# Latent attention over the prompt: transposes of a step ahead of the scores of the step three ahead

## The chip, the cores and the metric

The kernel runs on one core of one Trainium2 chip. The metric is the device time of one execution in microseconds (us); the kernel before takes 2766.6 us, the median of three runs (2764.68 to 2768.49).

## The reference, cut to what matters

The program is one inference step of a two-layer encoder: a layer with latent attention (MLA) and a layer with stick-breaking attention, each followed by an MLP. It works on a prompt of 1024 tokens and on 8 streams of 16 new tokens. The change touches only the latent attention over the prompt. For each of 8 heads it computes:

```
scale = (MLA_NOPE + MLA_ROPE) ** -0.5
s = (einsum('bqhd,bkhd->bhqk', q_nope, k_nope)
     + einsum('bqhr,bkr->bhqk', q_rope, k_rope)) * scale
mask = (k_pos[None, :] // CHUNK) <= (q_pos[:, None] // CHUNK)      # CHUNK = 64
s = where(mask, s, -inf)
p = softmax(s, axis=-1)
out = einsum('bhqk,bkhd->bqhd', p, v)
```

The outputs are float32. The kernel splits each float32 operand into a high and a low part, and a product is three matmuls (`product`, lines 77 to 79 of the kernel).

## The kernel before, in words

`mla_attention_stage` (line 582) handles the heads in four pairs, one pair per iteration of `pairs`. Within a pair there are `STEPS = 16` steps: step n is head n // 8 of the pair and query tile q = n % 8 of 128 tokens. Because of the mask, tile q needs only the first (q + 1) x 128 keys, so the steps grow from 128 to 1024 keys and start again at step 8. Each step passes through these pieces:

- **Scores** (`scores(n)`, TensorE, lines 923 to 938): three matmuls for the non-rotary part and two for the rotary part on each chunk of up to 512 keys, then one small matmul that adds the mask (L936). They are written to one of two score buffers, `score[n % 2]`, so `scores(n + 3)` first waits until the exponential of step n + 1 has read that buffer.
- **Maximum** (`maximum(n)`, VectorE, L838 and L841): the negated row maximum, and its product with the scale.
- **Exponential** (`exponential(n)`, ScalarE, L750): reads the scores, writes `prob[n % 3]`, and sums the rows.
- **Normalise** (`normalise(n)`, VectorE, L847 and L849): the reciprocal of the sum, and the probabilities times it, in place.
- **Transposes** (`transposes(n)`, TensorE, L946): they wait for `normed`, the signal of the normalise of the same step, and turn the q + 1 blocks of 128 x 128 in tasks of up to four into one of three banks. A task needs its bank emptied by the low split of the task three before.
- **High and low split** (ScalarE L761, VectorE L859): copy a task out of its bank into `pt`.
- **Values** (`values(g)`, TensorE, lines 950 to 959): once for every two steps (a group), 3 x (last_q + 1) matmuls of 256 columns, that is 6, 12, 18 and 24 for the four groups of a head; the result is copied out by ScalarE (L768).

Four value projections and `scores(0)` to `scores(2)` stand ahead of the 16 steps, and the projections of the next pair follow steps 13 to 15 (`TAIL`). At step 6 ScalarE and VectorE also split the raw weights of the next pair (L737, L742, L826, L831), in all pairs but the last.

Every engine runs its instructions in the order in which they are written, and the orders are written out by hand. On VectorE the loop over n is: `maximum(n + 3)`, `normalise(n + 1)`, the weights at step 6, `transposed_lo(n)`. On ScalarE it is: `exponential(n + 2)`, the weights at step 6, `transposed_hi(n)`, and the output of a group at even n. The change leaves both orders alone. SP's queue holds the stores of a group (L662), the loads of the next weights (L568, L570) and of the rotary queries (L656); GpSimd does nothing in this stage.

Of the kernel before, what the change touches and what calls it, by code (L numbers as in the profile page):

```python
# [74 lines left out]
def product(pe, out, w, m, start, stop, resumed=False):  # L75

    pe.matmul(out, w[0], m[0], start=start, stop=False, skip_group_check=resumed)  # L77
    pe.matmul(out, w[0], m[1], start=False, stop=False, skip_group_check=resumed)  # L78
    return pe.matmul(out, w[1], m[0], start=False, stop=stop, skip_group_check=resumed)  # L79
# [447 lines left out]
def score_columns(q):  # L527


    used = (q + 1) * P  # L530
    keys = max(used, 2 * P)
    first = P if keys == 640 else 0
    chunks, at = [], first
    while at < first + keys:
        end = min(512 * (at // 512 + 1), first + keys)
        chunks.append((at, end - at, at - first))
        at = end
    return first, chunks, used


def transpose_tasks(n):


    q = n % NPT
    order = [(q, 0)] + [(k, k + 1) for k in range(q)] if q % 2 else [(k, k + 1) for k in range(q + 1)]
    return [order[i:i + 4] for i in range(0, len(order), 4)]


def tasks_before(n):

    return sum(len(transpose_tasks(m)) for m in range(n))


STEPS = 2 * NPT
# [27 lines left out]
def mla_attention_stage(nc, io, scratch, raw, wq, smp_in, q_rope_out, o_out):  # L582
# [12 lines left out]
    with nc.cleanup_on_exit(), ExitStack() as ctx:  # L595
# [38 lines left out]
        def task_bank(m):  # L634

            return bank[:, 4 + m % 3, :]

        def project_bank(n):

            return bank[:, n % 4 if n < QK - 2 else 4 + n % 3, :]  # L640

        def pairs(engine, body):

            with engine.Fori(0, PAIRS - 1) as i:
                body(i, False)
            body(PAIRS - 1, True)
# [240 lines left out]
        @block.tensor  # L887
        def _(pe):
            proj.start(pe)
            pv_done.start(pe)  # L890

            def project(i, n, first=False):
                if n < 4 and not first:
                    exp_done.wait(pe, STEPS * i + n // 2 - 1)
                elif n >= 4:

                    reused = n - 4 if n < QK - 2 else n - 3 if n >= QK + 1 else None
                    if reused is not None:
                        proj_lo.wait(pe, PROJ * i + reused + 1)
                    elif n < QK:  # L900
                        t_lo.wait(pe, T_TASKS * i)
                ps = project_bank(n)
                if n < Q_TASKS:
                    a, c = n // 3, n % 3
                    for k in range(QT):
                        last = product(pe, ps[:, 0:384], [w[:, k, a, :] for w in wq],
                                       [x[:, k, c * 384:(c + 1) * 384] for x in cqT], k == 0, k == QT - 1)
                elif n < Q_TASKS + K_TASKS:
                    a, c = (n - Q_TASKS) // 2, (n - Q_TASKS) % 2
                    for k in range(CT):  # L910
                        last = product(pe, ps, [w[:, k, a, 0:NOPE] for w in wkv],
                                       [x[:, k, c * 512:(c + 1) * 512] for x in ckvT], k == 0, k == CT - 1)
                else:
                    for j in range(2):
                        t = 2 * (n - Q_TASKS - K_TASKS) + j
                        for k in range(CT):
                            last = product(pe, ps[:, j * GQ:(j + 1) * GQ],
                                           [x[:, k, t * P:(t + 1) * P] for x in ckvT],
                                           [w[:, k, :, NOPE:] for w in wkv], k == 0, k == CT - 1)
                last.then_inc(proj.sem, 1)  # L920

            def body(i, is_last):
                def scores(n):
                    a, q = n // NPT, n % NPT
                    tile = slice(q * P, (q + 1) * P)
                    exp_done.wait(pe, STEPS * i + n - 1)
                    first, chunks, used = score_columns(q)
                    for at, width, key in chunks:
                        out = score[n % 2][:, at:at + width]
                        keys = slice(key, key + width)  # L930
                        product(pe, out, [x[:, a, tile] for x in qn], [x[:, a, keys] for x in kn], True, False)
                        pe.matmul(out, qr[:, a, tile], krT[0][:, keys], start=False, stop=False)
                        last_chunk = (at, width, key) == chunks[-1]
                        last = pe.matmul(out, qr[:, a, tile], krT[1][:, keys], start=False, stop=not last_chunk)
                    end = first + used
                    last = pe.matmul(score[n % 2][:, end - P:end], io["ident16"][:], io["chunk_mask"][:],  # L936
                                     start=False, stop=True)
                    last.then_inc(s_done.sem, 1)

                def transposes(n):  # L940
                    normed.wait(pe, STEPS * i + n + 1)
                    for j, task in enumerate(transpose_tasks(n)):
                        m = tasks_before(n) + j
                        t_lo.wait(pe, T_TASKS * i + m - 2)
                        for c, (k, _) in enumerate(task):
                            last = pe.transpose(task_bank(m)[:, c * P:(c + 1) * P],  # L946
                                                prob[n % 3][:, k * P:(k + 1) * P], ident[:])
                        last.then_inc(t_done.sem, 1)

                def values(g):  # L950
                    a, last_q = g // 4, 2 * (g % 4) + 1
                    t_lo.wait(pe, T_TASKS * i + tasks_before(2 * g + 2))
                    o_done.wait(pe, GROUPS * i + g)
                    order = [(last_q, 0)] + [(k, k + 1) for k in range(last_q)]
                    for k, slot in order:
                        last = product(pe, bank[:, 7, 0:GQ],
                                       [x[:, k, a * VDIM:(a + 1) * VDIM] for x in v],
                                       [x[:, slot, :] for x in pt[g % 2]], k == last_q, k == last_q - 1)
                    last.then_inc(pv_done.sem, 1)

                proj_lo.wait(pe, PROJ * i + QK - 3)
                qr_in.wait(pe, 16 * (i + 1))
                scores(0)
                proj_lo.wait(pe, PROJ * i + QK - 2)
                scores(1)
                for n in range(QK, PROJ):
                    project(i, n)
                scores(2)
                for n in range(STEPS):
                    if n + 3 < STEPS:  # L970
                        scores(n + 3)
                    if n == 0:
                        proj_lo.wait(pe, PROJ * (i + 1))
                        zero_done.wait(pe, 4)
                    if n == NPT + 1:
                        values(NPT // 2 - 1)
                    transposes(n)
                    if n % 2 == 0 and n >= 2 and n != NPT:
                        values(n // 2 - 1)
                    if n == min(TAIL) and not is_last:  # L980
                        w_lo.wait(pe, 2 * (i + 2))
                    for m in TAIL.get(n, ()) if not is_last else ():
                        project(i + 1, m)
                values(GROUPS - 1)
                for m in TAIL[STEPS] if not is_last else ():
                    project(i + 1, m)

            w_lo.wait(pe, 1)
            for n in range(QK):
                if n == Q_TASKS:  # L990
                    w_lo.wait(pe, 2)
                project(0, n, True)

            pairs(pe, body)
    return w_four

# [1937 lines left out]
class SbSchedule:  # L2934
# [6 lines left out]
    STEPS = 2 * PAIR_STEPS  # L2941
# [798 lines left out]
```

## Time and profile before

| what | us |
|---|---|
| median of three runs | 2766.6 |
| the profiled execution's own time | 2768.86 |
| its span | 2765.2 |
| TensorE busy, whole span | 2667.1 (96%) |
| VectorE busy | 1733.0 (63%) |
| ScalarE busy | 1156.7 (42%) |

The span is what the profiler saw of one execution, from the first instruction of the program to the last; the time of the execution lies some 3.7 us above it. TensorE's busy time is of matmuls whose ends are modelled: a matmul is shown for longer than the distance to the next one, because they are pipelined. The latent attention over the prompt takes the stretch from 163 to 457 us of the span.

### The profile page before, as it was taken

The page shows a single profiled execution, that of the slowest core. Times are in us where ns is not written, and L with a number is a line of the kernel's source. Part 1 is how long each engine was busy: PE and PEld are TensorE (multiplying, and loading weights), DVE is VectorE, ACT ScalarE, POOL GpSimd, SP SyncE. Part 2 cuts the span into 40 slices and gives each one's busy share as a digit, 9 for nine tenths or more (in the row PEclk, how much of TensorE's full clock was granted, in tenths as well). Part 3 has the DMA queues.
Part 4 walks back from the last instruction along what each step waited for, and adds up shares of the span by engine and source line. Part 5 has one row for each costly group of instructions (what it writes and reads, how often), then busy time and mean ns, then how long its engine had stood idle before and what let it go on. Part 6 is the DMA issues. An engine that isn't in the chain of part 4 may idle for free. (4 is left out here: it accounts for less than half of the span.)

```text
span 2765.2 us, 40402 instructions
## 1 busy us (share of the span) xinstructions
PE 2667.1 (96%) x14531; PEld 2236.8 (81%) x14531; DVE 1733.0 (63%) x2331; ACT 1156.7 (42%) x2260; POOL 732.0 (26%) x627
## 2 busy tenths in 40 slices
PE   7989998999999999999899999998999999999998
PEld 6878887788888878888798887776878888788886
DVE  5656666376555688888410008887485555788887
ACT  4334445343333333344322219998343333333433
POOL 3200001135544400000221116666045544300001
PEclk9999999999999999999999999999999999999999
DMA  4211122514444573533234437763324444654342
GB/s 150 86 61 46 46 79 89 184 60 153 137 137 144 170 256 125 162 122 118 80 128 151 155 102 194 172 173 121 111 95 145 137 137 145 235 181 164 127 154 100
DMA packets 285877, 368.81 MB, mean 133 GB/s; under 512 B 25984, under 2 KB 205696, under 8 KB 285696
## 3 DMA queue, kind: packets, MB, share of 16 engines
q1 hardware_dynamic: 285696, 366.42, 41.7%
q8 instruction: 110, 1.80, 0.3%
q14 instruction: 71, 0.58, 0.1%
HBM read 242.19 MB, written 124.16 MB: 132 GB/s over the span
## 5 line engine op out<-in xcount | busy, mean ns | idle before, releaser
L2342 DVE TENSOR_TENSOR x<-m_ps,x 128x1024 f32<-128x1024 f32 x224 | 273.3, 1220 | 91.9 <-PE m_ps L79 91.8
L2051 POOL TENSOR_TENSOR m_u<-m_u,m_u 128x512 f32<-128x512 f32 x128 | 179.6, 1414 | 349.0 <-DVE m_u L2185 344.0
L1998 POOL TENSOR_SCALAR m_stat<-m_stat 128x1 f32<-128x1 f32 x36 | 12.1, 335 | 831.6 <-ACT m_sqjunk L1942 667.2
L2173 DVE TENSOR_TENSOR m_z<-m_ps,m_part 128x512 f32<-128x512 f32 x96 | 66.3, 691 | 143.8 <-PE m_ps L79 143.5
L1800 ACT COPY m_part<-m_ps 128x512 f32<-128x512 f32 x96 | 56.4, 588 | 205.2 <-PE m_ps L79 205.2
L2161 DVE TENSOR_TENSOR m_up<-m_upr,m_up 128x512 fp32r<-128x512 f32 x128 | 87.9, 707 | 28.5 <-ACT m_up L1787 28.5
L3300 ACT ACTIVATE e_b<-e_ps 128x512 f32<-128x512 f32 (+3 forms) x192 | 95.9, 500 | 12.1 <-PE e_ps L3518 11.6
L1787 ACT CAST m_up<-m_upr 128x512 fp32r<-128x512 f32 x128 | 75.7, 615 | 57.9 <-PE m_ps L79 57.9
L3302 ACT ACTIVATE e_ps<-e_ps 128x512 f32<-128x512 f32 (+3 forms) x192 | 96.3, 501 | 0.0
L2031 POOL TENSOR_TENSOR m_uprS<-m_upr 128x512 f32<-128x512 f32 x62 | 94.6, 1526 | 5.0 <-DVE m_upS3l L2161 4.9
L3583 PE MATMUL e_ps<-ident,e_b 128*128 128x128 f32 x576 | 94.7, 274 | 0.7 <-POOL e_b L3398 0.6
L2185 DVE SCALAR_TENSOR_TENSOR m_u<-m_z 128x512 f32<-128x512 f32 x96 | 90.1, 939 | 2.3
L2859 ACT COPY d_rows<-d_ps 128x512 f32<-128x512 f32 x36 | 21.1, 587 | 163.1 <-PE d_ps L79 163.1
L1138 POOL TENSOR_TENSOR c_wo0l<-c_wo0r,c_wo0h 128x1024 fp32r<-128x1024 f32 x1 | 2.4, 2352 | 322.5 <-ACT c_wo0h L1112 322.5
L2161 DVE TENSOR_TENSOR m_upS2l<-m_uprS,m_upS2h 128x512 fp32r<-128x512 f32 x32 | 33.9, 1061 | 84.7 <-ACT m_upS2h L1787 84.7
L77 PE MATMUL m_ps<-m_up,m_t8h 128*128 128x256 f32 x256 | 72.5, 283 | 0.9 <-DVE m_t8l L2123 0.9
L79 PE MATMUL m_ps<-m_up,m_t8l 128*128 128x256 f32 x256 | 72.4, 283 | 0.0
L78 PE MATMUL m_ps<-m_up,m_t8h 128*128 128x256 f32 x256 | 72.4, 283 | 0.0
L3583 PEld LDWEIGHTS e_ps<-ident,e_b 128*128 128x128 f32 x576 | 65.3, 141 | 6.8 <-ACT e_pt L3327 0.7
L3327 ACT COPY e_pt<-e_ps 128x512 f32<-128x512 f32 (+3 forms) x128 | 67.1, 524 | 0.0
L3398 POOL TENSOR_TENSOR e_b<-e_b,e_r0long 128x1024 f32<-128x1024 f32 (+3 forms) x32 | 53.8, 1682 | 42.0 <-DVE e_r0long L3454 41.9
L3398 POOL TENSOR_TENSOR e_b<-e_b,e_r1long 128x1024 f32<-128x1024 f32 (+3 forms) x32 | 53.3, 1666 | 43.8 <-DVE e_r1long L3454 43.8
(1192 smaller groups left out, 9185.8 us busy)
## 6 DMA issues: line engine op xcount, KB each, us to landing
scratch_u<-m_u SPq DMA_DIRECT2D x224, 256.0 KB, 2.1
m_ur<-scratch_u SPq DMA_DIRECT2D x208, 256.0 KB, 2.7
m_upr<-in_mlp_w_up SPq DMA_DIRECT2D x32, 1024.0 KB, 5.9
m_wr<-in_mlp_w_down SPq DMA_DIRECT2D x64, 512.0 KB, 6.6
scratch_x<-x SPq DMA_DIRECT2D x18, 512.0 KB, 2.6
x<-scratch_x SPq DMA_DIRECT2D x8, 1024.0 KB, 9.5
scratch_qr<-a_qrst SPq DMA_DIRECT2D x9, 512.0 KB, 3.4
a_x<-in_x_prompt SPq DMA_DIRECT2D x8, 512.0 KB, 5.0
```

Of the source, the lines that this page charges most:

```text
L77: pe.matmul(out, w[0], m[0], start=start, stop=False, skip_group_check=resumed)
L78: pe.matmul(out, w[0], m[1], start=False, stop=False, skip_group_check=resumed)
L1787: act.copy(up[n][0], up_source(n, p)).then_inc(up_hi.sem, 1)
L2031: pool.tensor_tensor(up_sum[n][:], up_source(ins[0], p), up_source(ins[1], p), ALU.add if n == "S1" else ALU.subtract).then_inc(up_summed. ...
L2051: pool.tensor_tensor(u_st[out][:], u_st[a][:], u_st[b][:], op).then_inc(u_summed.sem, 1)
L2161: dve.tensor_tensor(up[n][1], up_source(n, p), f32(up[n][0]), ALU.subtract).then_inc(up_lo.sem, 1)
L2185: dve.scalar_tensor_tensor(out=u_st[slot][:], in0=src[:], scalar=0.0, in1=src[:], op0=ALU.max, op1=ALU.mult).then_inc(u_done.sem, 1)
L2342: dve.tensor_tensor(out, bank[:, at:at + 2, :], out, ALU.add).then_inc(summed.sem, 1)
L3300: act.activation(take(n)[:, key:key + used], z[:, 0:used], ACT.Sigmoid, scale=SB_SCALE).then_inc(taken.sem, 1)
L3302: act.activation(z[:, 0:used], z[:, 0:used], ACT.Sigmoid, scale=-SB_SCALE).then_inc(kept.sem, 1)
L3398: pool.tensor_tensor(b, b, remaining(n)[:, -used:], ALU.mult).then_inc(weighted.sem, 1)
L3583: t = pe.transpose(task_bank(m)[:, c * P:(c + 1) * P], take(n)[:, k * P:(k + 1) * P], ident[:])
```

## The change: what it does

In TensorE's program, the call `scores(n + 3)` moves from the head of the loop body to behind `transposes(n)`. It then also comes behind the wait for the last value projection at n = 0 and behind `values(3)` at n = 9, and still ahead of `values(n // 2 - 1)` at the other even steps. No instruction is added or removed, and the order of no other engine changes.

```diff
                 scores(2)
                 for n in range(STEPS):
-                    if n + 3 < STEPS:
-                        scores(n + 3)
                     if n == 0:
                         proj_lo.wait(pe, PROJ * (i + 1))
                         zero_done.wait(pe, 4)
                     if n == NPT + 1:
                         values(NPT // 2 - 1)
                     transposes(n)
+                    if n + 3 < STEPS:
+                        scores(n + 3)
                     if n % 2 == 0 and n >= 2 and n != NPT:
                         values(n // 2 - 1)
                     if n == min(TAIL) and not is_last:
```

## Rows read from the trace of the kernel before

**Rows 1.** The page, part 1: busy time, share, and instructions of each engine.

```profile
PE 2667.1 (96%) x14531; PEld 2236.8 (81%) x14531; DVE 1733.0 (63%) x2331; ACT 1156.7 (42%) x2260; POOL 732.0 (26%) x627
```

**Rows 2.** Windows: stretch, length, engines' busy time (instructions), TensorE clock, DMA share, GB/s.

```profile
163.00:457.00 294.00, 285.31 (x1888) 259.51 (x1888) 183.49 (x419) 141.01 (x327) 0.00 (x0) 0.99 0.17 53
263.00:297.00 34.00, 32.97 (x225) 28.82 (x224) 26.32 (x65) 19.81 (x47) 0.00 (x0) 1.00 0.06 19
```

**Rows 3.** Waits of TensorE, 163 to 457: who for whom, total us, times, longest.

```profile
PE b_ps L77 <- ACT b_p L750: 2.6, 8, 0.4
...
PE b_ps L946 <- DVE b_p L849: 1.5, 5, 0.6
PE b_ps L946 <- DVE b_pt1l L859: 1.1, 3, 0.4
```

**Rows 4.** Timeline, end of scores(6), step 3: start, us, engine, line, operation, tiles, shape.

```profile
272.72 0.23 PE L936 MATMUL b_ps<-chunk_mask,ident 128*128 128x128 bf16 x1
272.78 0.60 PE L946 MATMUL b_ps<-ident,b_p 128*128 128x128 f32 x4
...
272.99 1.09 DVE L838 TENSOR_REDUCE b_stat<-b_ps 128x1 f32<-128x896 f32 x1 [0.94 <-PE b_ps L936]
...
274.11 0.15 DVE L841 TENSOR_SCALAR b_stat<-b_stat 128x1 f32<-128x1 f32 x1
274.19 0.15 DVE L847 RECIPROCAL b_stat<-b_stat 128x1 f32<-128x1 f32 x1
...
274.37 0.55 DVE L849 TENSOR_SCALAR b_p<-b_p,b_stat 128x640 f32<-128x640 f32 x1
...
274.84 0.69 DVE L859 TENSOR_TENSOR b_pt1l<-b_ps,b_pt1h 128x512 fp32r<-128x512 f32 x1
```

**Rows 5.** Timeline, step 13: a normalise and the transposes that waited for it.

```profile
301.34 0.62 DVE L849 TENSOR_SCALAR b_p<-b_p,b_stat 128x768 f32<-128x768 f32 x1
...
302.02 1.04 PE L946 MATMUL b_ps<-ident,b_p 128*128 128x128 f32 x6 [0.25 <-DVE b_p L849]
```

**Rows 6.** Lines by form, VectorE: busy us, mean ns, idle before; smallest and largest step.

```profile
L838 DVE TENSOR_REDUCE b_stat<-b_ps 128x1 f32<-128x1024 f32 x8 | 9.8, 1225 | 2.2 <-PE b_ps L936 2.2
...
L849 DVE TENSOR_SCALAR b_p<-b_p,b_stat 128x1024 f32<-128x1024 f32 x8 | 6.0, 754 | 0.3
...
L849 DVE TENSOR_SCALAR b_p<-b_p,b_stat 128x128 f32<-128x128 f32 x8 | 2.3, 287 | 0.3
L838 DVE TENSOR_REDUCE b_stat<-b_ps 128x1 f32<-128x128 f32 x8 | 2.3, 284 | 0.0
```

**Rows 7.** Timeline: the first matmul of values(1), and the first matmul after its twelve.

```profile
276.07 0.36 PE L77 MATMUL b_ps<-b_pt1h,b_vh 128*128 128x256 f32 x1
...
277.59 0.28 PE L77 MATMUL b_ps<-b_knh,b_qnh 128*128 128x256 f32 x1
```

**Rows 8.** Timeline, start of the second pair: scores(2) end, last low split, scores(4).

```profile
263.85 0.69 DVE L822 TENSOR_TENSOR b_vl<-b_ps,b_vh 128x512 fp32r<-128x512 f32 x1 [0.75 <-ACT b_vh L732]
...
263.91 0.23 PE L936 MATMUL b_ps<-chunk_mask,ident 128*128 128x128 bf16 x1
...
265.95 0.44 PE L77 MATMUL b_ps<-b_knh,b_qnh 128*128 128x384 f32 x1 [0.42 <-ACT b_p L750]
```

**Rows 9.** Timeline, steps 6 and 7: the weights on VectorE, and the transposes behind.

```profile
282.14 1.22 DVE L826 TENSOR_TENSOR b_wql<-raw_wq,b_wqh 128x1024 fp32r<-128x1024 f32 x1
283.27 1.22 DVE L831 TENSOR_TENSOR b_wkvl<-raw_wkv,b_wkvh 128x1024 fp32r<-128x1024 f32 x1
...
285.15 0.66 PE L946 MATMUL b_ps<-ident,b_p 128*128 128x128 f32 x4 [0.37 <-DVE b_pt1l L859]
```

**Rows 10.** Windows with idle in them; columns as in Rows 2.

```profile
20.00:25.00 5.00, 3.93 (x15) 3.24 (x16) 2.17 (x3) 1.24 (x2) 1.26 (x2) 0.75 0.90 203
30.00:35.00 5.00, 2.69 (x11) 2.22 (x12) 3.12 (x7) 2.36 (x7) 3.31 (x6) 0.78 0.02 3
...
456.00:460.00 4.00, 1.94 (x16) 1.73 (x16) 1.07 (x5) 1.96 (x5) 0.00 (x0) 1.00 0.44 118
```

## The prediction

> **What bounds the kernel now.** I read the page's busy times first, then the windows of the stage, then TensorE's waits in it, then one pair's timeline. TensorE is busy 96% of the span [rows 1], and the stage of the change is no exception: 285.3 of its 294 us [rows 2]. Between its steps TensorE hardly waits: eight waits for an exponential (2.6 us), five for a normalise (1.5), three for an emptied bank (1.1) [rows 3]. So this stage is bound by TensorE's own stream, at the full clock of 2.4 GHz, and whatever makes TensorE wait lengthens the kernel one for one. VectorE is the next busiest, 26.3 us in the 34 us of steps 0 to 12 of a pair [rows 2]. It has room in total, but what matters is when it gets to a normalise.
>
> The timeline shows why there are so few waits. At step 3 the last matmul of scores(6) starts at 272.72. VectorE starts maximum(6) when it has ended, and behind it in its queue normalise(4), which ends at 274.92 [rows 4]. TensorE has transposes(3), scores(7) and values(1) to do before it asks for normalise(4) in transposes(4). The 2 us of VectorE's chain lie beside more than 2 us of matmuls.
>
> **What the change does to that.** It adds and removes no instruction and no DMA; SP's queue and GpSimd are untouched. It moves scores(n+3) behind transposes(n), so after scores(n+3) the next thing that TensorE meets is transposes(n+1), with values between them at even n alone. But transposes(n+1) needs normalise(n+1), which stands in VectorE's queue behind maximum(n+3), which needs the end of scores(n+3). The cover is gone: TensorE finishes a step's scores and then stands still for VectorE's maximum and normalise. Queued behind the waiting transposes are scores(n+4) and all that follows them, and VectorE's next maximum waits for those, so the wait comes back at every step.
>
> **The price of one such wait**, counted from when TensorE could issue its next instruction:
> - 0.21 us until the maximum starts (272.78 to 272.99; the small matmul that ends the scores is still in the pipeline) [rows 4];
> - the maximum: 0.28 us for one tile of 128 keys, 1.23 for eight [rows 6], 0.134 for each tile between (the 1.09 for seven tiles fits [rows 4]);
> - 0.29 us from its end (274.08) to the start of the normalise, with the two small operations in it [rows 4];
> - the normalise: 0.29 us for one tile, 0.75 for eight [rows 6], 0.067 each between (0.55 for five fits [rows 4]);
> - 0.06 us from its end (301.96) to the transposes at 302.02 [rows 5].
>
> So 0.56 + maximum(n+3) + normalise(n+1). At even n the values matmuls are in front of it: twelve took 276.07 to 277.59, 0.127 us each [rows 7], so groups of 6, 12, 18 and 24 cover 0.76, 1.52, 2.28 and 3.04 us. Per pair:
> - n = 0, no values: 0.56 + 0.69 + 0.35 = 1.60
> - n = 1 and 9: 0.56 + 0.82 + 0.42 = 1.80 each
> - n = 2 and 10: 0.56 + 0.96 + 0.49 - 0.76 = 1.25 each
> - n = 3 and 11: 0.56 + 1.09 + 0.55 = 2.20 each
> - n = 4 and 12: 0.56 + 1.23 + 0.62 - 1.52 = 0.89 each
> - n = 5: 0.56 + 0.28 + 0.69 = 1.53
> - n = 6: 0.56 + 0.42 + 0.75 - 2.28, below zero: covered. n = 8 as well (1.60 against the 3.04 of values(3), which now stands directly behind scores(11)).
> - n = 7: 0.56 + 0.55 + 0.29 = 1.40
>
> These are 16.8 us a pair, 67.2 for four. From n = 13 on no scores are left, and nothing changes.
>
> **Smaller terms.** At n = 0 transposes(0) waits for the last value projection's low split, which ends at 264.54, while scores(2) is issued by 263.95 (the mask's matmul starts at 263.91) [rows 8]. Scores(3) covered this before; now it is 0.65 us, 2.6 for four pairs. Where a step has two tasks, the second needs the bank that the previous step's first low split empties; that split (0.69 us [rows 4]) now starts only behind the normalise that has just released the transposes, against 0.4 us for the first four of them: 0.25 us at steps 5, 6 and 13, 3.0 in all. At step 6 the weights (282.14 to 284.49, 2.35 us [rows 9]) stand between normalise(7) and that split. Normalise(7) ends 1.67 us after scores(9), the bank is free at 1.67 + 2.35 + 0.69 = 4.7, and TensorE is there at 2.28 + 0.4 = 2.7: 2.0 us in three pairs, 6.0.
>
> To be taken off: scores(4) and scores(9) no longer wait for an exponential, since the transposes now give it time. The rows have 2.6 us for these eight waits [rows 3]; to each I add 0.17 that the modelled end of the matmul ahead hides (0.23 less 0.06, [rows 4]) and, as an estimate, 0.1 for the start of a matmul that waited (0.44 us where one of 256 columns in the stream takes 0.28 [rows 7, 8]; part of that is its 384 columns): 4.8. The old waits at steps 7 and 13 are inside the new ones: 0.37 + 0.17 three times [rows 9] and about 0.4 four times [rows 5], 3.2 together. Off: 8.0.
>
> Sum at full clock: 67.2 + 2.6 + 3.0 + 6.0 - 8.0 = 70.8 us.
>
> **The clock.** The trace has stretches with idle in them at either level. From 20 to 25 and from 30 to 35 us the granted clock was 0.75 and 0.78, with TensorE busy 3.93 and 2.69 of 5 us; from 456 to 460 it stayed at 1.00 with 1.94 of 4 [rows 10]. The steps 0 to 12 of a pair will have some 33 us of matmuls in 52, with waits of up to 2.2 us, so both are possible. Bounds: no fall at all, nothing; the half clock of 1.2 GHz throughout these steps, 33 us more a pair less the 4.3 that longer values would hide, 115 us. A mean clock of 0.75 over 5 us is 2.5 us at half rate; with two thirds of such a stretch in matmuls, and counting a tail of it into the next one, a fall costs about 1.3 us. I take two or three a pair, near the 2.2 us waits and the pairs of 1.6 and 1.8: ten, 13 us. That is nearer to the lower bound, because most of the stretches between waits hold more work than the row that stayed at full clock.
>
> The Trainium skill has a rule that speaks against this change, in TensorE: Matmul & The Clock Gate, section "A second HAM failure mode: psum-queue depth-cycling": short idles of TensorE between groups of matmuls, when they come often, make the clock swing between its two levels. The sum would be 70.8 if it did not bite, and goes towards the upper bound if it did at each step; the trace of before has a stretch on either side, 0.75 and 1.00.
>
> Forecast: 2768.86 + 70.8 + 13 for the profiled execution; the median lies 2.3 below that execution, so 2766.6 + 84 = 2850 us.
>
> **The rivals.**
> - *Values cover every even step, and the bank waits are hidden.* Then only the odd steps pay: 1.80 + 2.20 + 1.53 + 1.40 + 1.80 + 2.20 = 10.9 a pair, 44 in all, 2810 us. For it: the even waits are what is left of a difference. Against: their parts are all measured.
> - *The clock is down in most of the steps.* 71 + 115 = 186 us, 2950. For it: rows at 0.75. Against: the row at 1.00 with half of the time idle.
> - *The other side: faster.* Scores(n+3) wait for the exponential of step n+1, and the transposes ahead of them give ScalarE time; the split of a step also starts earlier. If the transposes found their probabilities ready, the 8.0 us above were gained: 2759. The point from which it decides is 8.0 / 44, 0.18 us for each of the 11 waits of a pair; one alone of the five parts of a wait is 0.21. It would need the normalise to run ahead of the maximum on VectorE, and rows 4 show the written order.
> - *No change*, because a later stage takes the time up: it would need idle time of TensorE behind this stage that does not depend on it, and TensorE is 96% busy over the span [rows 1]. The 2767 of before.
>
> **How the numbers follow.** Forecast, whose own range is 2830 to 2870 (hardly any falls to some twenty of them), 0.76; even steps covered 0.11; clock down in most steps 0.06; faster 0.04; no change 0.03. The range that holds 8 in 10 runs from 2818, between forecast and first rival, to 2878. What can be told from no change here is about 0.2%, 5.5 us. Slower 0.93, same 0.03, faster 0.04.
>
> **What would show it.** The stage should be some 84 us longer and everything behind it as long as before. The waits of TensorE should have a new first row, transposes (L946) for the normalise (L849), with about 40 waits and 60 us, the longest near 2 us; the row for the exponential should be gone. In the timeline, at step 3, the end of scores(6), maximum, normalise and the transposes of step 4 should follow one another with no matmul beside them. VectorE's and ScalarE's busy time should be unchanged. The windows of the stage should show a mean clock between 0.9 and 1. The prediction is wrong if transposes(n+1) start less than 1 us after scores(n+3) at odd n, or if the stage grows by less than 50 us.

## The result

The changed kernel takes 2848.0 us (median of four runs, 2841.1 to 2851.5) against 2765.6 us of the kernel before in four runs: slower by 2.94%, ratio 1.0294 with a 95% interval of 1.0278 to 1.0309. The prediction was 2850 us, from 2818 to 2878. The profiled execution took 2851.5 us, its span 2848.1.

The windows show where the time went. First the kernel after: the stage of the change, the rest of the span, and 5 us inside the stage (length, busy PE, PEld, DVE, ACT, POOL, clock, DMA share, GB/s).

```profile
163.50:534.50 371.00, 298.47 (x1888) 266.44 (x1889) 184.28 (x419) 141.84 (x327) 0.00 (x0) 0.98 0.14 42
534.50:2848.10 2313.60, 2249.14 (x11896) 1862.50 (x11896) 1454.39 (x1761) 955.49 (x1802) 693.90 (x562) 0.99 0.45 145
...
285.40:290.40 5.00, 3.49 (x15) 3.23 (x14) 1.47 (x5) 1.20 (x4) 0.00 (x0) 0.66 0.00 0
```

The same two stretches of the kernel before:

```profile
163.30:457.50 294.20, 285.31 (x1888) 259.51 (x1888) 183.49 (x419) 140.71 (x327) 0.00 (x0) 0.99 0.17 53
457.50:2765.20 2307.70, 2244.42 (x11896) 1858.91 (x11896) 1454.35 (x1761) 956.05 (x1802) 693.85 (x562) 0.99 0.46 145
```

The stage is 76.8 us longer. VectorE and ScalarE are as busy as before in it. What follows it is 5.9 us longer in this pair of executions, but the same stretch took 2302.2 to 2314.5 us in the executions below, with no edit behind the stage, so these 5.9 us lie within what one execution differs from another and can't be put down to the change. A granted clock of 1.00 is 2.4 GHz, one of 0.50 is 1.2 GHz. The stage opens at the lower level in both kernels, behind a wait of 3.8 us before and 4.0 us after (L802): before from 163.3 to 169.3, after from 163.5 to 167.6. TensorE's waits in the stage (who for whom, total, times, longest) answer to [rows 3]:

```profile
PE b_ps L946 <- DVE b_p L849: 61.7, 45, 2.0
PE b_ps L946 <- DVE b_pt1l L859: 5.4, 3, 1.8
PE b_ps L77 <- DVEq L802: 4.0, 1, 4.0
PE b_ps L946 <- DVE b_vl L822: 2.1, 4, 0.5
```

The transposes now wait 45 times for the normalise, 61.7 us where it was 1.5; three times for the bank behind the weights, 5.4 us where it was 1.1; four times for the last value projection (L822), which is new. The wait at the stage's opening (L802) stood in the kernel before as well, and so did one of 1.6 us for the values of the last pair. The waits for an exponential are gone. The timeline at step 3 answers to [rows 4]:

```profile
299.15 0.23 PE L936 MATMUL b_ps<-chunk_mask,ident 128*128 128x128 bf16 x1
299.42 1.09 DVE L838 TENSOR_REDUCE b_stat<-b_ps 128x1 f32<-128x896 f32 x1 [2.48 <-PE b_ps L936]
300.54 0.15 DVE L841 TENSOR_SCALAR b_stat<-b_stat 128x1 f32<-128x1 f32 x1
300.61 0.15 DVE L847 RECIPROCAL b_stat<-b_stat 128x1 f32<-128x1 f32 x1
...
300.80 0.55 DVE L849 TENSOR_SCALAR b_p<-b_p,b_stat 128x640 f32<-128x640 f32 x1
...
301.41 0.76 PE L946 MATMUL b_ps<-ident,b_p 128*128 128x128 f32 x5 [2.03 <-DVE b_p L849]
```

End of scores(6), maximum(6), normalise(4), transposes(4): one after the other, and no matmul beside them. VectorE had sat idle for 2.48 us before the maximum, waiting for the scores; then TensorE sat idle for 2.03 us, waiting for VectorE. Before, the same normalise ran beside scores(7).

### The profile page after: what moved, and what is told of

Read it like the earlier page. It is cut to its first block and busy times, and to the rows that moved or that the text cites. A ratio compares the mean times of both kernels' runs of the same rounds, so it can differ in the third digit from the quotient of the medians.

```text
span 2848.1 us, 40402 instructions
## 1 busy us (share of the span) xinstructions
PE 2685.0 (94%) x14531; PEld 2247.3 (79%) x14531; DVE 1734.0 (61%) x2331; ACT 1157.0 (41%) x2260; POOL 731.1 (26%) x627
## 5 line engine op out<-in xcount | busy, mean ns | idle before, releaser
L946 PE MATMUL b_ps<-ident,b_p 128*128 128x128 f32 x288 | 47.7, 287 | 69.2 <-DVE b_p L849 61.7
L838 DVE TENSOR_REDUCE b_stat<-b_ps 128x1 f32<-128x128 f32 (+3 forms) x64 | 48.4, 757 | 103.9 <-PE b_ps L936 103.9
L946 PEld LDWEIGHTS b_ps<-ident,b_p 128*128 128x128 f32 x288 | 31.4, 141 | 79.9 <-DVE b_p L849 41.5
L750 ACT ACTIVATE b_p<-b_ps,b_stat 128x128 f32<-128x128 f32 (+3 forms) x64 | 47.5, 742 | 70.8 <-DVE b_stat L841 70.7
```

The lines of the kernel that those rows point to most:

```text
L946: last = pe.transpose(task_bank(m)[:, c * P:(c + 1) * P], prob[n % 3][:, k * P:(k + 1) * P], ident[:])
```

## The experiments

Each was compared with runs of the kernel before on the same chip; the ratio is to those.

**Is the wait the place in VectorE's queue?** e1 is the changed kernel with two calls swapped:

```diff
-                    if n + 3 < STEPS:
-                        maximum(n + 3)
                     if n + 1 < STEPS:
                         normalise(n + 1)
+                    if n + 3 < STEPS:
+                        maximum(n + 3)
```

> The changed kernel with VectorE's two calls swapped: normalise(n+1) ahead of maximum(n+3); the low split stays last. Theory (TensorE stands still because the normalise is queued behind the maximum of the scores just issued): the 45 waits of transposes for the normalise, 61.7 us, all but vanish. What is left to pay is the low split, still behind the maximum: second tasks of steps 5, 6, 7 and 13 wait for their bank and values(3) for its operands, about 13 us in all, with 2.6 us for the last value projection; 8 us of old waits are gone. So 2769 to 2778. Rival 1 (the clock and the move of the scores themselves cost the time): stays above 2835. Rival 2 (ScalarE, whose exponential now stands between, is what is late): the transposes keep waiting and half or more of the 82 us stays, above 2805.

Measured: 2774.9 us, ratio 1.0031 (1.0018 to 1.0044). The first waits of TensorE in the stage of e1:

```profile
PE b_ps L77 <- DVE b_pt1l L859: 4.6, 5, 1.6
PE b_ps L946 <- DVE b_pt0l L859: 4.6, 13, 0.6
PE b_ps L77 <- DVEq L802: 4.0, 1, 4.0
PE b_ps L946 <- DVE b_pt1l L859: 3.0, 3, 1.0
```

The 61.7 us of waits for the normalise are down to one of 0.6. TensorE's program is the changed one, so neither the move itself nor a late exponential makes the time, nor does the clock fall behind the stage's opening: it is the maximum ahead of the normalise. The remaining 0.3% are waits for the low split (L859), which is still behind the maximum, as expected.

**The swap without the change.** e3 is the kernel before with the same swap.

> The kernel before (scores ahead of transposes) with VectorE's normalise(n+1) ahead of maximum(n+3): the swap alone, as a control for the two above. Theory: the chain behind the scores had its cover there, so the swap is worth next to nothing, within 4 us of 2766 (at most the 1.5 us of waits for a normalise). If the swap were a gain of its own, whatever TensorE's order, it would be here too: 10 us or more below 2766.

Measured: 2767.7 us, ratio 1.0007 (0.9997 to 1.0016). The swap is worth nothing that can be measured where the chain had its cover. It undoes a wait; it is no gain of its own.

**The length of the wait.** e5 is the changed kernel, e6 the one before, both with

```diff
-dve.tensor_reduce(stat[:, n, 0:1], score[n % 2][:, first:first + used], AX.X, ALU.max,
+dve.tensor_reduce(stat[:, n, 0:1], score[n % 2][:, first:first + P], AX.X, ALU.max,
```

> The changed kernel with the maximum taken over the first 128 keys of each row only (the rest of the row is left out of the maximum, nothing else): each maximum costs 0.28 us instead of up to 1.23. Theory: every wait shrinks by what its maximum shrinks: 0.41, 0.54, 0.68, 0.81, 0.89, 0, 0.27, 0.54, 0.68, 0.81 and 0.89 us, 6.5 a pair, 26 in all, so 2822, and the waits for the normalise fall from 61.7 to about 36 us. Rival (a wait has a fixed price, of the handover between engines or of the clock): within 8 us of 2848.

> The kernel before with the same shortened maximum (first 128 keys of each row; the rest is left out of it). Theory: there the maximum lies beside matmuls and is not on the path, so it is worth only the few waits for an exponential: 2760 to 2767. Rival (VectorE's total work counts in this stage): 15 us or more below 2766.

Measured: e5 2810.2 us (1.0160, 1.0140 to 1.0181), e6 2761.6 us (0.9981, 0.9972 to 0.9991). The stage and the first wait of e5:

```profile
162.90:501.50 338.60, 290.30 (x1888) 261.01 (x1889) 154.84 (x419) 140.02 (x327) 0.00 (x0) 1.00 0.15 46
```

```profile
PE b_ps L946 <- DVE b_p L849: 37.2, 37, 1.4
```

About 30 us less of VectorE's work were worth 38 us in the changed kernel and 5 in the one before: the maximum is on the path only with the new order. The waits shrank by 24.5 us, close to the 26 that was forecast; the time shrank by 12 more than forecast. The stage accounts for 32.4 (371.0 to 338.6): the 24.5; some 6 us of clock, by the price below, since behind the stage's opening the changed kernel's clock fell four times and that of e5 never; and 0.6 us, as e5's opening stretch at 1.2 GHz was 2.9 us long instead of 4.1. About 1 us is left open. The rest of the 38 lies outside the stage and is within the spread named above.

**The cover of the values.** e4 puts values ahead of scores(n+3) in the changed kernel.

```diff
                     transposes(n)
-                    if n + 3 < STEPS:
-                        scores(n + 3)
                     if n % 2 == 0 and n >= 2 and n != NPT:
                         values(n // 2 - 1)
+                    if n + 3 < STEPS:
+                        scores(n + 3)
```

> The changed kernel with values ahead of scores(n+3) at even n too, so that nothing lies between scores and the next transposes but at n = 8. Theory (a wait is 0.56 + maximum + normalise less the values in between): at n = 2, 4, 6, 10, 12 the cover of 0.76, 1.52, 1.73, 0.76 and 1.52 us is taken away, 6.3 us a pair or 25 in all, and the values wait some 0.2 us for the low split ahead of them: 28 us over the changed kernel, about 2876, and the waits of transposes for the normalise grow from 61.7 to about 87 us. Rival (the even steps' waits come from something else than this difference, such as the clock): within 10 us of 2848.

Measured: 2897.7 us, ratio 1.0480 (1.0463 to 1.0498), 22 us more than expected. The stage and the first wait of e4:

```profile
163.10:589.40 426.30, 328.15 (x1889) 294.11 (x1889) 184.29 (x420) 144.74 (x327) 0.00 (x0) 0.89 0.12 36
```

```profile
PE b_ps L946 <- DVE b_p L849: 86.1, 49, 2.2
```

The waits came out as worked out, 86.1 us for the 87 forecast: the values matmuls take their own length off a wait. The surplus is the clock, which the expectation left out. Its mean in the stage is 0.89 instead of 0.98: added up over windows of 0.5 us, TensorE spent 96 us at its lower level instead of 18. The stage grew by 55.3 us over the changed kernel, 24.4 of them this wait and 1.2 the wait for the bank; some 30 us are left for 78 more us at 1.2 GHz, nearly 0.4 us each. TensorE's busy time says the same: 328.2 us for the matmuls that took 298.5. (What follows the stage was the shortest of all here, 2302.2 us, so the time shows less than the stage.)

**Only some of the steps.** e7 and e8 put scores(n+3) behind transposes(n) at the odd and at the even steps alone.

```diff
+                    if n + 3 < STEPS and n % 2 == 0:     # e8: n % 2 == 1
+                        scores(n + 3)
                     transposes(n)
-                    if n + 3 < STEPS:
+                    if n + 3 < STEPS and n % 2 == 1:     # e8: n % 2 == 0
                         scores(n + 3)
```

> The change at the odd steps only: scores(n+3) behind transposes(n) at odd n, ahead of them at even n. Behind every odd step then come the scores of the even one, so normalise(n+1) has those beside it; only transposes(n+1) at even n still come soon, behind scores(n+3), transposes(n) and values. Theory: waits of transposes for the normalise at steps 1, 3, 5, 11 and 13 alone, 1.2 + 0.8 + 0.2 + 0.8 + 0.2 us a pair, 13 us in all, and the exponential's waits of before go; 2775 to 2784, no falls of the clock in the stage. Rival (each step at which transposes stand ahead of the scores costs its share of the 82 us, here seven of thirteen): 2805 or more.

> The change at the even steps only: scores(n+3) behind transposes(n) at even n, ahead of them at odd n (behind values(3) at n = 9). Theory: each even step's scores are followed by values and by the next scores, so those waits are covered; but the scores of an odd step n have only transposes(n) between them and transposes(n+1): waits of 1.43, 1.6, 0.7, 0.4, 1.43 and 1.6 us at steps 2, 4, 6, 8, 10 and 12, 7.1 a pair, 29 in all, and 2.6 us for the last value projection; 2790 to 2801. Rival (each step costs its share, here six or seven of thirteen): 2804 to 2810, and waits at the odd steps as well.

Measured: e7 2796.2 us (1.0112, 1.0091 to 1.0133), e8 2807.5 us (1.0147, 1.0128 to 1.0165). Both are above the upper end of their expectation, e7 by 12 us and e8 by 6. e7 lies between its expectation and its rival; e8's time lies in its rival's range (2804 to 2810), so the time alone does not decide, and the waits have to. Their first wait, e7 and then e8:

```profile
PE b_ps L946 <- DVE b_p L849: 17.3, 25, 1.4
```

```profile
PE b_ps L946 <- DVE b_p L849: 34.4, 29, 1.6
```

These were 13 and 29 in the expectations. In the second pair of e7 the steps 1, 3, 5, 11 and 13 wait 1.39, 0.76, 0.29, 0.77 and 0.29 us where 1.2, 0.8, 0.2, 0.8 and 0.2 were given, but step 6 waits 0.73 us too: scores(9), which I took for cover, have 256 keys and are too short. The weights' bank wait of [rows 9] grew from 0.37 to 1.33 us, and values(3) wait 0.87 us for the low split. In the second pair of e8 the steps 2, 4, 6, 8, 10 and 12 wait 1.36, 1.59, 1.01, 0.93, 1.41 and 1.59 us where 1.43, 1.6, 0.7, 0.4, 1.43 and 1.6 were given. Of the odd steps, which the rival has waiting too, 1, 3, 5, 7, 9 and 11 do not wait for the normalise; step 13 does, 0.75 us, and the formula gives it (0.89 less 0.17, see below), but I had left it out. Each of the two also has one fall of the clock in the stage where the expectation of e7 had none. So single waits can be worked out from a formula, but for the two at steps 6 and 8 of e8; the list of who waits was not complete. Time is also not proportional to the number of steps that are changed: what counts is what stands between the scores and the next transposes.

**Can the followers follow?** In e2 VectorE takes the low split ahead of the maximum as well. In e9 ScalarE moves its high split too, and in e10 e9's orders of ScalarE and VectorE meet TensorE's old one. The diff is e9's against the changed kernel; e2 has only the second half of it, with weights_lo ahead of the split.

```diff
 # ScalarE
-                    if n + 2 < STEPS:
-                        exponential(n + 2)
-                    if n == WEIGHTS_AT and not last:
-                        weights_hi(i + 1)
                     if n == NPT + 1:
                         output(NPT // 2 - 1)
                     transposed_hi(n)
+                    if n + 2 < STEPS:
+                        exponential(n + 2)
+                    if n == WEIGHTS_AT and not last:
+                        weights_hi(i + 1)
 # VectorE
-                    if n + 3 < STEPS:
-                        maximum(n + 3)
                     if n + 1 < STEPS:
                         normalise(n + 1)
-                    if n == WEIGHTS_AT and not last:
-                        weights_lo(i + 1)
                     transposed_lo(n)
+                    if n + 3 < STEPS:
+                        maximum(n + 3)
+                    if n == WEIGHTS_AT and not last:
+                        weights_lo(i + 1)
```

> The changed kernel with VectorE's order normalise(n+1), weights at step 6, transposed_lo(n), maximum(n+3). Theory: neither the transposes nor their banks wait for a maximum any longer; the exponential's waits of before (4.8 us) stay gone, the projection's 2.6 us stay. Something like 2758 to 2768, level with the kernel before or a little under it. Rival 1 (clock or the move itself): above 2835. Rival 2 (the maximum, now late behind the split, delays the exponential and with it the scores): a new wait of scores for the exponential of some 1 us at the short steps 5 to 8, 2770 to 2785.

> The changed kernel with all three followers in TensorE's new order: ScalarE takes transposed_hi(n) ahead of exponential(n+2), VectorE takes normalise(n+1), transposed_lo(n), maximum(n+3), and both take the weights of step 6 last. The trace of e2 showed VectorE idle for the high split (up to 0.96 us), which stood behind an exponential that itself waited for the delayed maximum. Theory: with the split ahead of the exponential that loop is cut; no transposes wait for a normalise or a bank, 2.6 us stay for the last value projection, the 4.8 us of waits for the exponential are gone: 2758 to 2768, level with before or a little under it. Rival (the loop is not what held e2 up; the scores' exponential is now late): 2775 or more, with scores waiting for the exponential.

> The kernel before (scores ahead of transposes on TensorE) with the same new orders on ScalarE and VectorE. The transposes, and with them the splits, come later there, and the maximum waits behind them. Theory: the maximum, and through it the exponential of the scores two ahead, loses its lead of some 2 us; a few waits of scores for the exponential at the short steps 6 to 9: 2765 to 2778, not under e9. Rival (the follower orders are a gain whatever TensorE's order): 2760 or less, and level with e9.

Measured: e2 2783.4 us (1.0054, 1.0034 to 1.0074), 15 us above its expectation. The time is in rival 2's range, but rival 2's wait is not there: no scores wait for an exponential. This is step 5 and 6 of e2's second pair:

```profile
278.45 1.01 ACT L750 ACTIVATE b_p<-b_ps,b_stat 128x896 f32<-128x896 f32 x1 [1.94 <-DVE b_stat L841]
...
279.45 0.74 ACT L761 CAST b_pt0h<-b_ps 128x512 fp32r<-128x512 f32 x2
280.06 0.89 DVE L859 TENSOR_TENSOR b_pt0l<-b_ps,b_pt0h 128x512 fp32r<-128x512 f32 x2 [0.92 <-ACT b_pt0h L761]
...
280.87 1.22 DVE L838 TENSOR_REDUCE b_stat<-b_ps 128x1 f32<-128x1024 f32 x1
...
283.19 0.65 PE L946 MATMUL b_ps<-ident,b_p 128*128 128x128 f32 x4 [1.28 <-DVE b_p L849]
```

The maximum waits for the low split, that for the high split, which stands behind an exponential that had waited for the maximum one step earlier: ScalarE and VectorE hand one another the turn, and the normalise behind them is late. e9 cuts this: 2765.9 us, ratio 0.9994 (0.9985 to 1.0004). With TensorE's new order the stage is back to the old time, 291.4 us in its trace (1.2 us of the 2.8 under the old 294.2 come from an opening stretch at 1.2 GHz of 3.7 us instead of 6.0). Its waits:

```profile
PE b_ps L946 <- DVE b_vl L822: 2.1, 4, 0.5
...
PE b_ps L77 <- DVE b_pt1l L859: 1.6, 1, 1.6
PE b_ps L946 <- DVE b_p L849: 1.4, 4, 0.4
PE b_ps L946 <- DVE b_pt0l L859: 0.4, 1, 0.4
```

e10 went the other way: 2820.9 us, ratio 1.0188 (1.0175 to 1.0202), over 40 us above its expectation.

```profile
PE b_ps L77 <- ACT b_p L750: 48.3, 44, 1.8
```

Here it is the scores that stand still, 44 times, for the exponential; in the order as it is written, the maximum now comes behind the splits of transposes that TensorE reaches only behind the next scores. The clock fell four times, too. I had seen these waits at four steps and taken the lead of 2 us for enough at the others. e10 is the mirror image of the change: the orders of three engines fit each other or they don't. No version that takes the whole maximum beat the kernel before beyond what can be measured; e6, which leaves a part of it out, did by 0.2%.

## Why the prediction was right

**The bound and the mechanism.** Right. The lost time is TensorE idle for the normalise, and e1 removes it by moving that one call.

**The price of a wait.** Right to 0.1 us, once a difference in counting is taken off. The trace counts idle from the modelled end of the mask's matmul, 0.17 us later than the formula. In the second pair the waits of transposes(1) to transposes(6) were 1.51, 1.71, 1.15, 2.03, 0.75 and 1.44 us; the formula less 0.17 gives 1.43, 1.63, 1.08, 2.03, 0.72 and 1.36. Transposes(7) and (9) did not wait for the normalise, as said. Sum: 67.2 less 44 x 0.17 is 59.7, and 61.7 less the one old wait at the end of the last pair (0.55) is 61.2. One reading of the prediction was wrong and did not enter the sum: it had values(1) among the matmuls ahead of transposes(4) in the kernel before. They stand behind them (transposes(4) start at 275.60, values(1) at 276.07 [rows 7]), so the old cover of normalise(4) was transposes(3) and scores(7), from 272.78 to 275.60, 2.8 us beside a chain that ended at 274.92.

**The smaller terms.** The projection at n = 0: 2.1 us of idle, 2.8 with the 0.17 each; 2.6 was given. The bank behind the weights: 5.4 + 3 x 0.17 = 5.9; 6.0 was given. The other bank waits (3.0) do not show as idle, but the stream of transposes has them in part. At step 5 the six transposes are shown longer than before, first the kernel before, then the one after:

```profile
278.26 0.82 PE L946 MATMUL b_ps<-ident,b_p 128*128 128x128 f32 x6
306.76 1.04 PE L946 MATMUL b_ps<-ident,b_p 128*128 128x128 f32 x6 [0.75 <-DVE b_p L849]
```

That is 0.22 us, 0.05 of which every group of transposes that had waited shows (four blocks take 0.41 us to the next matmul instead of 0.36). At step 13 the six took 1.04 us before and after [rows 5], and at step 6 nothing was added. So these bank waits cost under 1 us in all and not 3.0; the slower start of 44 waiting groups, 0.05 us each and about 2 us in all, is a term that the prediction did not have, and that the two are as large as the 3.0 is chance. The exponential's waits went, as said.

**The clock** was the term off in size. Four short falls came in the stage behind its opening, one a pair, where I took ten. One is in the windows above, 0.66 from 285.4 to 290.4. From transposes(1) to the mask's matmul of scores(4) took 3.15 us with it (287.17 to 290.32) and 1.74 in the last pair without (470.31 to 472.05): 1.4 us, where I had 1.3 a fall. The steps with the four falls, each from the start of its transposes to the next that waited, took 1.6, 1.5, 1.5 and 1.6 us longer than the same step of a pair without one. So some 6 us instead of 13. The same matmuls of scores(4) in the two pairs, second and last:

```profile
287.17 0.68 PE L946 MATMUL b_ps<-ident,b_p 128*128 128x128 f32 x2 [1.51 <-DVE b_p L849]
...
287.97 0.52 PE L78 MATMUL b_ps<-b_knl,b_qnh 128*128 128x384 f32 x1
...
290.32 0.30 PE L936 MATMUL b_ps<-chunk_mask,ident 128*128 128x128 bf16 x1
...
470.31 0.44 PE L946 MATMUL b_ps<-ident,b_p 128*128 128x128 f32 x2 [1.43 <-DVE b_p L849]
...
470.76 0.34 PE L78 MATMUL b_ps<-b_knl,b_qnh 128*128 128x384 f32 x1
...
472.05 0.23 PE L936 MATMUL b_ps<-chunk_mask,ident 128*128 128x128 bf16 x1
```

The stage's growth less this is about 71 us, against the 70.8 of the sum at full clock; the shorter opening stretch at 1.2 GHz (4.1 us instead of 6.0) hides 1 us more. That the median still came within 2 us of the forecast is chance: the 7 us too many for the clock stand against the 6 us by which the rest of the span was longer in this pair of executions.

The rule that I cited from the Trainium skill (TensorE: Matmul & The Clock Gate, "A second HAM failure mode: psum-queue depth-cycling") holds in kind: frequent short idles made the clock swing, four times here and to a mean of 0.89 in e4. With the same kind of waits, but none for the normalise over 1.4 us (and three for a bank of up to 1.7), e5 had no fall behind the stage's opening. That is no threshold: e7, with fewer such waits and none over 1.4 us either, had one. What decides whether a given wait brings a fall stays open.

**The rivals.** "Values cover every even step" is out: steps 3, 5, 11 and 13 waited, and e4 moved the waits by the values' own length. "Clock down in most steps" did not come here, but e4 shows its beginning. The faster one was right that the exponential's waits go; with transposes that find their probabilities ready (e9) its gain still did not show in the time: 0.9985 to 1.0004 against the 0.997 that it had.

## What to carry to other kernels

Moving an operation on the engine that bounds the kernel also moves it past what other engines have queued: look for the operand's producer in its engine's queue, and at what stands ahead of it there. Here the normalise, whose result the transposes need, was queued behind the maximum, which needs the scores that had been moved right ahead of those transposes. The cost was latency plus both durations, less whatever matmuls stayed in between. If such an order is changed, change all of its followers together and read the waits of each engine: with one or two of the three orders moved the cost was 0.3% (e1), 0.5% (e2), 1.9% (e10) and 2.9% (the change), with all three nothing (e9).

## What the runs showed of the hardware

- TensorE's clock did not fall, behind the stage's opening, with 37 waits of up to 1.4 us for the normalise (e5, 37.2 us in all); it fell once a pair with 45 of up to 2.0 us (the changed kernel, 61.7 us), once a pair with 44 of up to 1.8 us for the exponential (e10, 48.3 us), and was down for over a fifth of the time, 96 of 426 us, with 49 of up to 2.2 us (e4, 86.1 us). The total of the waits does not order the runs: e7 with 25 (17.3 us) and e8 with 29 (34.4 us) had one fall each, and e2, with 15.2 us in 13 waits for normalise and bank, had one twice as long as the others. Each of these counts is from one profiled execution.
- The price was about 0.4 us per us at 1.2 GHz (0.4 to 0.5 for the falls of the changed kernel, nearly 0.4 in e4) and not the full half. A part of that time is waits for VectorE, which ends its work no later for it; that this makes the difference is argued, not tested.
- A few more waits can so cost more than their length: e4's 24 us of added waits came with about 30 us of slower clock.
